# Two transformer blocks on one core: the first product tiles behind each norm take x times its weight, the root is applied at their eviction, and five conditioning slabs change place

## The reference

```python
def rms(x, g):
    y = x32 * lax.rsqrt(jnp.mean(x32 * x32, axis=-1, keepdims=True) + EPS)
    return (y * g).astype(x.dtype)

ada = c_act @ w_ada[l] + b_ada[l]                  # six vectors of 1024 per layer
sh1, sc1, gt1, sh2, sc2, gt2 = split(ada, 6)
h = rms(x, g_mix[l]) * (1.0 + sc1) + sh1
parts = h @ w_in[l]                                # q, k, v of two attentions, gate_a, gate_b
...
x = x + gt1 * (mixed @ w_out[l])
h2 = rms(x, g_mlp[l]) * (1.0 + sc2) + sh2
x = x + gt2 * (jnp.square(jax.nn.relu(h2 @ w_ff1[l])) @ w_ff2[l])
```

## Time and profile before

| what | us |
|---|---|
| median of 3 runs | 2291.45 (2289.05 to 2291.9) |
| the profiled execution, device time | 2291.23 |
| its span in the trace | 2289.4 |
| PE busy in the span | 2249.8 |
| POOL busy | 1691.9 |
| DVE busy | 1259.3 |
| ACT busy | 632.8 |

### The profile page before, as it was taken

How to read it: one execution, slowest core, us unless ns; L and a number is a source line. 1 busy time by engine, 2 the same in 40 slices (tenths; PEclk the granted TensorE clock), 3 DMA queues, 4 the chain that set the end, 5 groups by cost and what they waited for, 6 DMA issues and landing times.

```text
span 2289.4 us, 31094 instructions
## 1 busy us (share of the span) xinstructions
PE 2249.8 (98%) x11693; PEld 1828.1 (80%) x11693; DVE 1259.3 (55%) x1798; ACT 632.8 (28%) x1286; POOL 1691.9 (74%) x2678
## 2 busy tenths in 40 slices
PE   8999999999999999999999999999999999999999
PEld 6888677788887888777778888878877777888887
DVE  7986345554446665544867576457554456723221
ACT  3233344332224111543223233111144421300000
POOL 7998170867888798344889887889853387899884
PEclk9999999999999899999999999999999999999999
DMA  7456741334455332111545555533321132433221
GB/s 204 129 137 153 268 151 35 116 101 159 159 186 186 111 111 94 50 36 39 164 131 189 174 191 177 184 107 97 100 79 33 29 124 92 154 107 107 92 92 56
DMA packets 268656, 280.87 MB, mean 123 GB/s; under 512 B 29964, under 2 KB 240592, under 8 KB 268508
## 3 DMA queue, kind: packets, MB, share of 16 engines
q1 hardware_dynamic: 249756, 245.86, 34.8%
q10 hardware_dynamic: 18752, 33.03, 4.3%
HBM read 257.87 MB, written 17.85 MB: 120 GB/s over the span
## 4 chain that ended last, share of the span: by engine, by line
PE 85%; POOL 6%; DVE 4%; issue 2%; ACT 2%; DMA 1%; SPq 0%; ACTq 0%; DVEq 0%; POOLq 0%
PE ps L496 46%; PE ps L674 14%; PE ps L2527 4%; PE ps L2528 4%; PE ps L2529 4%; POOL ring_low L272 4%; POOL ring_high L268 3%; PE ps L982 2%; PE ps L1025 2%; PE ps L1001 2%; PE ps L1175 1%; PE ps L1182 1%; PE ps L1158 1%; PE ps L2637 1%; DVE ada_acc L408 1%
## 5 line engine op out<-in xcount | busy, mean ns | idle before, releaser
L272 POOL TENSOR_TENSOR ring_low<-ring,ring_high 128x256 fp32r<-128x256 f32 x1309 | 1039.0, 824 | 28.4
L268 POOL TENSOR_SCALAR ring_high<-ring 128x256 fp32r<-128x256 f32 x1309 | 609.1, 491 | 478.3 <-PE ps L674 170.8
L496 PE MATMUL ps<-hT_high,ring_high 128*128 128x512 f32 x704 | 278.0, 395 | 1.4 <-DVE hT_low L860 1.4
L496 PE MATMUL ps<-hT_low,ring_high 128*128 128x512 f32 x704 | 274.9, 390 | 0.0
L496 PE MATMUL ps<-hT_high,ring_low 128*128 128x512 f32 x704 | 274.0, 389 | 0.0
L674 PE MATMUL ps<-hT_high,ring_high 128*128 128x512 f32 x568 | 234.5, 413 | 3.2 <-POOL ring_low L272 1.4
L674 PE MATMUL ps<-hT_high,ring_low 128*128 128x512 f32 x568 | 225.3, 397 | 0.0
L674 PE MATMUL ps<-hT_low,ring_high 128*128 128x512 f32 x568 | 225.1, 396 | 0.0
L408 DVE TENSOR_REDUCE ada_acc<-ring 128x256 f32<-128x2048 f32 x48 | 188.8, 3933 | 54.8 <-ACT ring L395 54.7
L496 PE MATMUL ps<-hidden_high,ring_high 128*128 128x512 f32 x512 | 201.0, 393 | 0.0
L496 PE MATMUL ps<-hidden_low,ring_high 128*128 128x512 f32 x512 | 199.6, 390 | 0.0
(11 more groups left out here) (401 smaller groups left out, 4030.5 us busy)
## 6 DMA issues: line engine op xcount, KB each, us to landing
ring<-in_w_in_dram SPq DMA_DIRECT2D x75, 1024.0 KB, 5.3
ring<-in_w_ff_dram SPq DMA_DIRECT2D x64, 1024.0 KB, 5.4
ring<-in_w_ada_dram SPq DMA_DIRECT2D x48, 1024.0 KB, 5.4
ring<-in_w_out_dram SPq DMA_DIRECT2D x12, 1024.0 KB, 5.8
scratch_x<-xT ACTq DMA_DIRECT2D x3, 2048.0 KB, 8.2
ring<-in_w_mem_kv_dram SPq DMA_DIRECT2D x4, 1024.0 KB, 5.4
ring<-in_w_branch_a_dram SPq DMA_DIRECT2D x16, 256.0 KB, 4.0
xT<-scratch_x ACTq DMA_DIRECT2D x2, 2048.0 KB, 9.7
```

What stands on the lines that cost most here:

```text
L268: ins = nc.gpsimd.tensor_scalar(x(hi), x(raw), 1.0, 1.0, ALU.mult, ALU.mult)
L272: ins = nc.gpsimd.tensor_tensor(x(lo), x(raw), x(hi).bitcast(F32), ALU.subtract)
L496: return nc.tensor.matmul(out[0:rows, bank, cols[0]:cols[1]], lhsT, rhs, start=start, stop=stop)
```

## The change

1. The gains of a norm are made ahead, in the stage before it, and as each k of x is added, ACT writes x times its gain into `hT_high` and DVE the rest into `hT_low` (`Unnormed`), with no root and no shift.
2. `norm_stage` runs the first tiles on that: one tile of the MLP at norms B and D, the two tiles of the first gate slab (`m{l}0ga`) at norms A and C. The turn of the sums and the spreading of the root stand between their k. `warm` goes. Then two-column matmuls of each weight half with the shift (`shift_two`) make the shift's share of the tile. DVE multiplies the tile by the root when it is evicted; ACT applies the shift as bias.
3. `hT` is then overwritten with the normed x as before, for all other tiles; ACT waits for each k until PE has used the old content (`unnormed_used`).
4. The slab `m{l}0ga` moves ahead of the qkv slabs, and the stream has 14 tiles in place of 16, with shorter pace lists.
5. Five of the 24 `w_ada` slabs of layer 0 move into the merge, between `g` and `p` of pairs 1, 3, 5, 7 and 9 (pairs counted from 0): two come from the first out stage, three from layer 0's out stage.

```diff
-    def ada(l):
+    def ada(l, half=1):
...
-        key = (last, 1) if K.slabs[last][3] else (last, None)
+        key = (last, half) if K.slabs[last][3] else (last, None)
...
             add(f"merge{mp}{b}g", w, dm, O_GL + D * b, D, part=mp)
+            one = (len(K.slabs) - 1, 1)
+            if (3 * mp + b) % 2 and mp < 3 or (mp, b) == (3, 0):
+                ada(0, 0)
             add(f"merge{mp}{b}p", T[pw][0], (0, rows), 0, D, part=mp)
...
         add("out", T["w_out"][0], dm, 0, D, part=i)
-        ada(0)
+        if i < 2:
+            ada(0)
     for l in range(LAYERS):
         w2 = T["w_in_2"][l]
+        add(f"m{l}0ga", w2, dm, 3072, D, part=0)
...
             add(f"out{l}", T["w_out_2"][l], dm, 0, D, part=i)
-            if l == 0 and i < 3:
-                ada(0)
```

The new class, and the new body of `norm_stage` on PE (the branch of norm A, with its two roots, left out):

```diff
+class Unnormed:
...
+    def round_up(self, e, k):
+        K = self.K
+        K.nc.scalar.activation(K.hT[0][:, k, :], self.src[:, k, :], ACT.Copy, scale=self.gain[:, k:k + 1]
+                               ).then_inc(self.high.sem, 1)
+
+    def low_part(self, e, k):
+        K = self.K
+        e.wait_ge(self.high.sem, self.base + k + 1)
+        K.nc.vector.scalar_tensor_tensor(K.hT[1][:, k, :], self.src[:, k, :], self.gain[:, k:k + 1],
+                                         K.hT[0][:, k, :].bitcast(F32), ALU.mult, ALU.subtract).then_inc(self.low.sem, 1)
...
+            pe.wait_ge(taken.sem, taken.total - 2)
+            for k in range(KD):
+                products_of(k)
...
+                else:
+                    if k == (2 if len(tiles) == 1 else 1):
+                        pe.wait_ge(taken.sem, taken.total)
+                        turn(turn_bank, (sums, last))
+                    if k == (5 if len(tiles) == 1 else 3):
+                        pe.wait_ge(inverted.sem, i0 + 1)
+                        spread_root(root_bank, 4)
+            for n, t in enumerate(tiles):
+                for k in range(KD):
+                    for x in (3 * k, 3 * k + 2):
+                        ins = nc.tensor.matmul(ps[:, shift_bank, 2 * n:2 * n + 2], t[x][3], K.shift_two[:, k, :],
+                                               start=x == 0, stop=x == 3 * KD - 1)
+                ins.then_inc(made.sem, 1)
...
             def round_up(k):
                 e.wait_ge(scaled.sem, s0 + k + 1)
+                e.wait_ge(used.sem, u0 + k + 1)
...
+            for n in range(len(tiles)):
+                K.link(e, "dve_step", v.tensor_reduce(K.shift_of[:, n:n + 1], ps[:, shift_bank, 2 * n:2 * n + 2], AX_X, ALU.add))
+                take(e, n, ps[:, tile_banks[n], :], rstd[:, :])
```

And the paces of the stream (wide attention's are shortened in the same way), with the wait that `qkv_stage` gets on PE at its second group:

```diff
+                if g == 1:
+                    pe.wait_ge(*gates_scaled)
...
-                    [72 + 9 * i for i in range(18)] + [240, 252])
+                    [72 + 8 * i for i in range(18)] + [216, 226])
```

More of the change, by code:

```diff
@@ L438, in tiles_stage @@
 def tiles_stage(K, tiles, banks, act=None, dve=None, act_on=None, after=None, entry=None, arriving=None, tensor_entry=None, act_lead=4,
-                also=None, ahead=None, ada_bank=7, late=None, entry_at=None, waits=None, ada_lead=2, ada_lag=3, back=None):
+                also=None, ahead=None, ada_bank=7, late=None, entry_at=None, waits=None, ada_lead=2, ada_lag=3, back=None, done=0):
     nc, ps = K.nc, K.ps
@@ L499, in _ @@
             if arriving is not None:
-                first = 2
+                first = 2 + done
                 size = len(tiles[0])
@@ L751, in norm_stage @@
+def norm_stage(K, src, gain, dst, shift, sums, last, unnormed, tiles, places, made, take, twice=None):
     nc, v, ps = K.nc, K.nc.vector, K.ps
-    first, second, third = banks
-    others = (0, 1, 6, 7)
+    tile_banks, turn_bank, root_bank, shift_bank, other_bank = places
     K.rms_count += 1
     c = K.rms_count
-    outer_rstd = K.region(f"rstd{c}", [P, SEQ], 53248)
+    outer_rstd = K.region(f"outer_rstd{c}", [P, SEQ], 53248)
+    rstd = K.region(f"rstd{c}", [P, SEQ], 55296)
     tmp = K.region(f"normed{c}", [P, 2, SEQ], 57344)
@@ L765, in norm_stage @@
+    t0, o0, i0, w0, c0, s0, h0, l0, u0 = (g.total for g in (turned, root, inverted, spread, copied, scaled, high, low, used))
+    taken, outer = K.sig("tile_taken"), K.sig("outer_normed")
+    made0 = made.total
     if twice is None:
@@ L2606, in qkv_stage, with turn_stage @@
     K.close(tensor=MA, scalar=VT, vector=DO)
-def turn_stage(K, turn, stream, paces):
+def turn_stage(K, turn, stream, paces, turn_gates, gates_turned):
     nc, ps = K.nc, K.ps
```

228 lines of the change are left out of this document (148 added, 80 removed).

## The result

The kernel after took 2316.79 us (median of 4 runs, 2315.17 to 2320.4), the kernel before 2291.53 beside it: a ratio of 1.0119 with an interval of 1.0106 to 1.0132. The change makes the kernel 25 us slower, where no difference was forecast (2290.6, range 2276 to 2302). The profiled execution of after spans 2315.4 us, 26.0 more than before's 2289.4.

The account below looks back on a forecast made before the run. PE was taken as the bound, busy 98% of the span with 85% of the chain. From 2291.2, gains of 22.3 were subtracted, 20.5 for the merge and 1.2 for the clock added: 2290.6 us, range 2276 to 2302.

Parts of the forecast that it names:

- the clock: At norms A and C: two-column matmuls might let the clock fall, 2.4 us per fall, one chance in four each: 1.2.
- rival 2: Merge: ACT waits for late w_ada slabs, delaying DVE and PE's transposes; five pairs cost 1 to 2 more each; 2300, chance 0.20.
- the overlap of the extra work in the first out stage: Out stages: extra ACT and DVE work, under 1 us each per tile, lies beside 5.4 us tiles; first out stage -0.8.
- the price of a turn: Norms: 8 one-column matmuls take 0.95 us at B, C and D; two turns of 12 take 2.9 at A.
- The slabs in the merge: Merge: five added slabs delay projection and gate slab loads, 8.2 + 15.5 + 3.6 less 6.8 absorbed: 20.5 us lost.
- What would show it: Merge: PE waits for ring_low of several us would support the forecast sum; PE waits for ada would support rival 2.
- Norm A: Norm A with two gate tiles: 20.4 us after, against 15.2 + 2.4 + 10.9 before, a gain of 8.1.
- Norms B, C and D: PE lists of 20.1 us at B and D, 16.3 at C; gains of 4.4 at B, 1.2 at C, 4.5 at D.
- Layer 0's out stage: Layer 0's out stage without three w_ada slabs: PE regains 2.2 us and three pairs of transposes go, a gain of 3.3.
- A matmul of two columns: Shift matmuls at the norms: 0.119 us each, taken from the one-column turn's records with the same 128 weight columns.
- rival 3: Shift matmuls at the norms: two-column matmuls cost only 0.068 us each, 96 taking 6.5 instead of 11.4; 2285.7, chance 0.10.
- the 10.9 us of the two moved gate tiles: Attention stage at norms A and C: PE is the bound, so 48 products leaving the stream come back in full, 10.9.

Follow-up runs that it names:

- the spare loads: The kernel before with five more loads in the merge, where the change puts its w_ada slabs, touched by no engine: 2312.57 us, ratio 1.0088.
- the exchange: Pair's own w_ada slab issued behind the next gate slab, in before with five untouched extra loads (2323.64 us) and in after (2337.03 us).
- after_wide: The kernel after with one-column turns widened to 64 columns and shift matmuls to 128: 2306.20 us, ratio 1.0065 against before.
- norm_only: The kernel after with w_ada slabs placed as in before, except layer 0's out-stage three, put in layer 0's mix: 2307.43 us, ratio 1.0067.

## Why the prediction was wrong, step by step

The steps that failed, by size: the clock (+1.2 in the sum, 9.2 measured), the merge (6.3 over its term, 4.7 of it the work on the slabs, which stood only in rival 2), the overlap of the extra work in the first out stage (3.8), and the price of a turn (0.9 at B, C and D, 2.3 at A). In detail:

- **The slabs in the merge** (+20.5; measured +26.8). The mechanism was right, and the sum near: the spare loads cost 22.1, with POOL's waits of 8.3 and 5.1 where 8.2 and 5 stood, 28.1 more of its waits for loads in all (27.3) and 5.6 less for PE (6.8). What reached PE as a wait is 13.5 of it, though, and the sum had no term for the clock in the merge, so that the two agree this well is in part luck. As for the rule of the Trainium skill on ring order (DMA: Bandwidth & Descriptors, Queues, rings and completion order), the exchange bears out what I read from it: with nothing ahead in the queue the gate slab's wait was 2.04. But in both kernels with the exchange the merge was longer and not shorter, so the place in the queue is not by itself what the slabs cost. Missing was the price of ACT, DVE and PE on these slabs, rival 2 (4.7, where it had 5 to 10 for the five pairs). Rival 2 had its place exactly (PE at the transposes of the sums), but as an addition. It takes the place of the waits for POOL, and only the excess counts.
- **What would show it.** I had `ring_low` waits of PE as the sign of my own sum and `ada` waits as that of the rival. After shows almost none of the first (1.7 in the merge) and 17.4 of the second, while the loads alone, the cause in my sum, cost 22.1 of the 26.8. A sign that names the waiting instruction does not tell which supply is late.
- **The first out stage** (-0.8; measured +3.0). The failed step is "the extra ACT and DVE work in the out stages lies beside tiles of 5.4 us on which DVE has some 3 to work". That is true of the layers' out stages (43.52 in both), not of the first: two sums of squares of 0.84, a residual of 1.06, the low part of 1.17 and its wait for ACT make 5.7.
- **Norm A** (-8.1; measured -2.6). Its own time was 24.7, not 20.4, and 4.0 of that is the clock: with wide matmuls it is 20.65. In that 20.65 the errors of my list cancel: no wait for the gate slab's split (1.5 less), spreadings of 0.35 where 0.65 stood (0.6 less), shift matmuls of 0.110 (0.3 less), and turns of 5.2 where 2.9 stood, counted too low as at B, C and D.
- **Norms B, C and D.** The list of PE had 8 one-column matmuls per turn for 0.95, read from the 8 records of the earlier trace rows. But these 8 records are the 4 matmuls of one operand, `squares_summed`: each stands as two records. A turn goes over `squared` too, 8 matmuls and 16 records; after has them from 1186.22 to 1188.03, 1.8 us. That is 0.9 at each. At C, which took 17.1 where 16.3 stood, the turn took 1.7 and the spreading 0.35 (0.65 in the list). At B the third tile was done after 22.6 us (forecast 20.1): besides 0.9 for the turn, DVE's pass over `hT` took 1.5 to 1.8 per k where two tiles together need 1.4, so it did not stay ahead of PE. B then lost 1.1 more to a wait for POOL in the MLP.
- **The clock** (+1.2; measured 9.2). This is the worst step. I had priced it by what the one fall at A in before cost behind the norm, 2.4, with a chance of 1 in 4 at two places. All six traces with the new norm and narrow turns show a fall at A, and all five with narrow shift matmuls one at C (326.2 to 327.8 us up to the mix, against 324.7 with wide ones, so 1.5 to 3.1 each). Against after_wide, after is 4.0 longer in norm A and 1.2 behind it, 2.9 at C and behind it and 1.1 at D, 9.2 in all. At B and D it is a matter of the execution: with the new norm and narrow turns the clock fell at B in three of seven traces and at D in five of eight, for up to 1.1 each (at B the third tile is done after 23.7 us instead of 22.6), and with wide turns in none of three. After has the fall at D and not at B.
- **What held.** Layer 0's out stage, -3.3. A matmul of two columns, 0.119 forecast and 0.110 measured where the clock held (32 in 3.51 us in norm_only), 0.121 in norm C of after; rival 3 falls. That the price came out near is in part luck: it was read from records of a matmul that stands as two. The 10.9 us of the two moved gate tiles come back in full: from qkv to the mix of layer 1 before took 318.9 and after_wide 308.0.

Together, of a miss of 26.6 in the traces: 6.3 in the merge, 3.8 in the first out stage, 8.0 for the clock at the norms beyond its term, 2.5 of chance ahead of the merge, and the 6.0 that are left for turns, DVE's pass and the wait in the MLP. What stays open is why the clock falls at B and D in some executions and not in others with the same list; no run was made for it.

## What to carry to other kernels

Count a ring of slots by what passes through it in one turn: where the loop of load, use and release has no slack in the trace, a load more costs its full share, 4.4 to some 7 us here in three stages, and in the one where both were tried a load of an eighth of the length still cost 3.7 of 4.4, and another order made it worse. Price an engine in the stage where it has most to do, not in the typical one. And where PE is kept "busy" with matmuls of one or two columns between full ones, make them wide: it cost nothing here, and gave 10.6 us with the new norm and nothing in the median with the old one, where PE also stood idle.

## What the chip showed that was not expected

TensorE's granted clock fell from the 2.4 to the 1.2 GHz level in stretches with hardly a gap in PE's work: at norm C among 32 matmuls of 2 columns (PE busy 17.10 of 17.10 us), and at norm A between two turns of one-column matmuls and behind the second (24.54 of 24.60). At C in after, up to the fall and behind it:

```profile
1559.77:1562.83 3.06, 3.06 (x30) 3.06 (x28) 2.99 (x5) 1.61 (x3) 0.00 (x0) 1.00 0.45 175
1562.83:1569.60 6.77, 6.77 (x20) 5.51 (x20) 6.57 (x14) 1.65 (x3) 5.53 (x9) 0.50 0.27 103
```

With 128 and 64 columns in the same matmuls it stayed at 1.00 in both. By the Trainium skill (TensorE: Matmul & The Clock Gate, Part 1: The HAM clock gate) the gate follows how busy TensorE has been; these runs show that the profile's busy time is not the measure of it, since it was 100% at C and over 99% at A in after and in after_wide alike, and only the columns differed. A matmul with 128 weight columns took 0.110 us with 2 moving columns and with 128, at the 2.4 GHz level.
